# Hybrid retention / RG-LRU trunk: a new opening, a recurrent stage with input gates first, and seams freed tile by tile

## What is computed

```python
for l in range(2):
    sh1, sc1, g1, sh2, sc2, g2 = split(silu(cond) @ mod_w[l] + mod_b[l], 6)
    h = rmsnorm(x, norm_mix[l]) * (1 + sc1) + sh1
    if l == 0:   # four heads of bidirectional retention and a chunked spatial-gating MLP
        q, k, v, g, u, vv = split(h @ ab_w_in)
        mix = concat([o_ret, o_gm]) @ ab_w_out
    else:        # bidirectional RG-LRU, eight blocks of 128 channels
        gate_in, x_in = split(h @ lru_w_in, 2)
        xc = centred_dwconv(x_in)                       # 4 taps along the tokens
        r, ig = sigmoid(xc @ wa + ba), sigmoid(xc @ wx + bx)      # for each direction
        a = exp(-8 * r * softplus(-lam))
        h_d = scan(a, sqrt(1 - a * a) * (ig * xc))      # h[t] = a[t] h[t-1] + b[t]
        mix = (gelu(gate_in) * (h_f + h_b)) @ lru_w_out
    x = x + g1 * mix
    h = rmsnorm(x, norm_mlp[l]) * (1 + sc2) + sh2
    x = x + g2 * (square(relu(h @ mlp_w1[l])) @ mlp_w2[l])
y = rmsnorm(x, final_norm)
```

## Time and profile before

| | us |
|---|---|
| median of 3 runs | 2721.26 (2720.76 to 2726.55) |
| profiled execution, its own time | 2729.32 |
| its span | 2727.5 |
| PE busy | 2606.4 (96%) |
| DVE busy | 1641.2 (60%) |
| ACT busy | 666.5 (24%) |
| POOL busy | 700.0 (26%) |

### The profile page before, as it was taken

One profiled execution on the slowest core, in us unless ns is written; L12 is line 12 of the kernel. 1 busy time (PEld: TensorE's weight loads), 2 busy tenths in 40 slices (PEclk: granted clock), 3 DMA queues, 4 the chain that ended last, 5 costly groups with the idle time before them and its releaser, 6 DMA issues.

```text
span 2727.5 us, 39975 instructions
## 1 busy us (share of the span) xinstructions
PE 2606.4 (96%) x14730; PEld 2519.9 (92%) x14730; DVE 1641.2 (60%) x3056; ACT 666.5 (24%) x1016; POOL 700.0 (26%) x395
## 2 busy tenths in 40 slices
PE   8999999899999999999999889789999999999998
PEld 4999999899999999999998778678999999999998
DVE  5778778548567567567586776865433433343444
ACT  5323323232001001001044545423110110110113
POOL 0211212222222222222223232332223222232221
PEclk9999999999999999999999889899999999999999
DMA  6422222312222222222222101121111111111111
GB/s 229 149 74 68 83 64 74 124 47 64 65 81 69 63 83 69 62 85 69 62 74 104 38 19 38 44 84 39 43 43 39 46 38 46 38 39 46 38 46 70
DMA packets 259139, 181.18 MB, mean 66 GB/s; under 512 B 9205, under 2 KB 253685, under 8 KB 258166
## 3 DMA queue, kind: packets, MB, share of 16 engines
q1 hardware_dynamic: 257924, 169.99, 20.3%
q10 hardware_dynamic: 1138, 10.21, 1.0%
HBM read 165.48 MB, written 14.69 MB: 66 GB/s over the span
## 4 chain that ended last, share of the span: by engine, by line
PE 84%; DVE 10%; issue 3%; ACT 2%; DMA 0%; ACTq 0%; DVEq 0%; POOL 0%; POOLq 0%; SPq 0%
PE psum L588 79%; PE psum L862 2%; DVE mod_sum L1228 2%; DVE work_f L1624 1%; DVE h_lo L1254 1%; DVE sumsq L1197 1%; PE mod_psum L613 1%; DVE x L1275 1%; PE psum L668 1%; DVE sumsq L1260 1%; DVE h_hi L1598 1%; DVE mod_sum L1223 0%; DVE s_bwd L1474 0%; PE psum L743 0%; ACT rate_f L1107 0%
## 5 line engine op out<-in xcount | busy, mean ns | idle before, releaser
L588 PE MATMUL psum<-h_hi,w_hi 128*128 128x384 f32 (+1 forms) x2880 | 678.5, 344 | 37.1 <-DVE h_lo L1254 26.5
L531 POOL CAST w_hi<-w_raw 128x1024 fp32r<-128x1024 f32 x184 | 194.1, 1055 | 1881.6 <-PE psum L588 1028.0
L588 PE MATMUL psum<-h_lo,w_hi 128*128 128x384 f32 (+1 forms) x2880 | 663.1, 339 | 0.0
L588 PE MATMUL psum<-h_hi,w_lo 128*128 128x384 f32 (+1 forms) x2880 | 662.8, 338 | 0.0
L588 PEld LDWEIGHTS psum<-h_hi,w_hi 128*128 128x128 f32 x2880 | 517.9, 190 | 49.2 <-issue 23.1
L1275 DVE SCALAR_TENSOR_TENSOR x<-psum,mod,x 128x768 f32<-128x768 f32 (+2 forms) x432 | 238.5, 610 | 476.4 <-PE psum L588 476.4
L588 PEld LDWEIGHTS psum<-h_lo,w_hi 128*128 128x128 f32 x2880 | 521.9, 190 | 0.0
L588 PEld LDWEIGHTS psum<-h_hi,w_lo 128*128 128x128 f32 x2880 | 521.2, 190 | 0.0
L533 POOL TENSOR_TENSOR w_lo<-w_raw,w_hi 128x1024 fp32r<-128x1024 f32 x184 | 445.3, 2420 | 14.7
L978 ACT ACTIVATE relu<-relu,bias 128x384 f32<-128x384 f32 x128 | 72.0, 610 | 1207.5 <-DVE relu L1326 1207.5
L588 PE MATMUL psum<-hid_hi,w_hi 128*128 128x384 f32 x1536 | 351.9, 336 | 2.8 <-DVE x L1275 2.8
(11 more groups left out here) (223 smaller groups left out, 1888.5 us busy)
## 6 DMA issues: line engine op xcount, KB each, us to landing
w_raw<-in_mlp_w SPq DMA_DIRECT2D x128, 512.0 KB, 4.0
mod_raw<-in_mod_w SPq DMA_DIRECT2D x160, 256.0 KB, 2.9
w_raw<-in_ab_w_in SPq DMA_DIRECT2D x24, 512.0 KB, 4.6
x_spill<-x ACTq DMA_DIRECT2D x2, 4608.0 KB, 13.9
w_raw<-in_lru_w_in SPq DMA_DIRECT2D x16, 512.0 KB, 4.3
x<-x_spill SPq DMA_DIRECT2D x2, 2880.0 KB, 9.3
x_rows<-in_x_sample SPq DMA_DIRECT2D x8, 512.0 KB, 7.6
scale_raw<-in_mod_w SPq DMA_DIRECT2D x8, 512.0 KB, 14.4
```

The costliest lines, as they stand in the source:

```text
L531: pool.tensor_copy(w_hi[:, s, :], w_raw[:, s, :]).then_inc(hi_done, 1)
L588: mm = pe.matmul(psum[:, s, c, 0:end - c * CH], w, v[:, k, c * CH:end], start=(first and n == 0 and w is hi[k] and v is in_hi), stop=(last ...
```

## The change

Three parts change together.

1. Opening. PE begins with 10 matmuls on a tile of ones; SP loads four row blocks ahead of the parameters; rows are transposed as they land, with the parameters' transposes (`PAR_ITEM`) after the fifth. Squares are summed along rows on ACT (`row_squares`) and turned into `rstd` by three matmuls (`spread_rstd`) in place of seven adds and three long reciprocals on DVE. The modulation rows are multiplied with a 32-wide conditioning tile into four strips of 32 PSUM rows (`row_half`), scale in two halves ahead of the first unit, shift inside it after tile 5. `h_hi` and `h_lo` are made directly from `x` (`first_high`, `first_low`).
2. Recurrent stage. PE runs X of blocks 0 and 1 first, and then for each b: gates of b, G of b, X of b+2. The gates come as input gates of both directions, then recurrence gates. The products of gate and input move from POOL to DVE; one subtraction moves from DVE to ACT, beside the root. The last block has its gates ahead of the last G.
3. Seams. `mod_col(7)` of a head runs after the next head's first unit, or inside `out_proj(0)`. In the last unit before a seam PE signals each tile of `h` that it has passed (`free=`), and ACT, DVE and POOL overwrite that tile for the next stage at once. The MLP's `h` is written directly from `x` (`high_direct`, `low_direct`), without `gained`.

```diff
-            for n in range(2):
-                pe.wait_ge(par_landed[n], 16 * len(par_loads[n::2]))
+            keep_busy(WARM)
+            pe.wait_ge(consts_landed, 16)
+            for n in range(PAR_ITEM):
+                turn_rows(n)
...
+            def row_half(item, c, weights):
+
                 for k in range(KT):
+                    q = WIDE * (k % 4)
+                    last = pe.matmul(psum[q:q + WIDE, item % 2, c, :], cond_wide[:, k, :], weights(k), start=(k < 4), stop=(k >= 4))
+                return last
...
+                        if k == KT - 2:
+                            take_set(None, 0, SHIFT_ITEM)
+                            for m in range(KT):
+                                pe.wait_ge(shift_landed[m], 16)
+                            row_half(SHIFT_ITEM, 0, lambda m: shift_raw[m][:, 0:HALF * P])
+                            row_half(SHIFT_ITEM, 1, lambda m: shift_raw[m][:, HALF * P:KT * P]).then_inc(mini_done, 1)
...
                 big(0, 0).then_inc(unit_done, 1)
+                if not first_head(h):
+                    mod_column(h, HEAD_MODS, M0 - 1)
                 big(1, 1).then_inc(unit_done, 1)
...
-                mod_col(7)
...
+            project(None, 0, I1, 0, U1, *norm_waits(2)).then_inc(unit_done, 1)
+            project(None, 0, I1 + 1, 0, U1 + 1).then_inc(unit_done, 1)
+            with pe.Fori(0, KT - 2) as b:
+                gates(b)
+                project(b, BLK_ITEMS, I1 + BLK_G, BLK_UNITS, U1 + 2).then_inc(unit_done, 1)
+                project(b, BLK_ITEMS, I1 + BLK_NEXT_X, BLK_UNITS, U1 + 3).then_inc(unit_done, 1)
+            gates(KT - 2)
+            project(KT - 2, BLK_ITEMS, I1 + BLK_G, BLK_UNITS, U1 + 2).then_inc(unit_done, 1)
+            gates(KT - 1, True)
+            project(None, 0, I1 + LAST_G, 0, U1 + 2 * KT - 1, free=h_passed).then_inc(unit_done, 1)
...
+            def high_direct(n, k):
+
+                if k == 0:
+                    act.wait_ge(gain_ready, n + 2)
+                for t, c in tokens(x[:, k, :]):
+                    act.activation(h_hi[:, k, c * LAT:c * LAT + t.shape[1]], t, ACT.Copy, scale=gain[:, k, c:c + 1])
+                act.activation(h_hi[:, k, TOK:COLS], mod[:, n // 2, (SH1, SH2)[n % 2] + k, :], ACT.Copy).then_inc(part_hi, 1)
...
-                act.wait_ge(unit_done, AT_MLP[l].units)
                 for k in range(KT):
-                    if k == 4:
+                    if k < KT - 1:
+                        act.wait_ge(out_passed, l * (KT - 1) + k + 1)
...
-                    high_part(norm, k)
+                    high_direct(norm, k)
...
+                if last_head:
+                    act.wait_ge(gm_out, HEADS)
+                    for k in MIX_ORDER[0][:EARLY]:
+                        act.wait_ge(heads_passed, k + 1)
+                        mix_part(k)
...
+                act.wait_ge(scanned, at(b, 2, 2))
+                for j, (d, kind) in enumerate(GATE_ORDER):
...
+                    if j == 1 and not last_block:
+                        conv_bias(b, BLK_X)
...
+                if last_head:
+                    for n in range(EARLY_DVE):
+                        low_part(MIX_ORDER[0][n], mix[:, MIX_ORDER[0][n], :], H_MIX[0], n, TOK)
                 unit(5)
```

More of the change, by code:

```diff
@@ L106 @@
 DVE_LOW = 2
+EARLY_DVE, EARLY = 3, 6
 class Steps:
@@ L577, in take_set, with three_passes @@
                 return c % 2
-            def three_passes(s, tiles, hi, lo, in_hi, in_lo, width=TOK, first=True, last=True, before=None, behind=None):
+            def three_passes(s, tiles, hi, lo, in_hi, in_lo, width=TOK, first=True, last=True, before=None, behind=None,
+                             free=None):
                 for n, k in enumerate(tiles):
@@ L1030, in _, with head @@
             I0, U0, M0 = AT_MIX[0].items, AT_MIX[0].units, AT_MIX[0].minis
-            with act.Fori(0, HEADS) as h:
-                steps.enter(h, 9)
+            def head(h, last_head):
+                steps.enter(None if last_head else h, 9)
                 def mini(n):
@@ L1083, in _ @@
                 act.activation(by_bank(tile_of(mix, h)), whole(s), ACT.Copy).then_inc(read_out[s], 1)
-            steps.leave(HEADS)
+                steps.leave(1 if last_head else HEADS - 1)
+            with act.Fori(0, HEADS - 1) as h:
+                head(h, False)
+            head(HEADS - 1, True)
             out_proj(0)
@@ new lines, in mix_low, with lru_block @@
+            def mix_low(start, end):
+                for k in range(start, end):
+                    low_part(k, mix[:, k, :], H_MIX[1], k, TOK)
+            def lru_block(b, more):
+                steps.enter(b if more == 2 else None, 14 if more else 8)
+                for d in range(2):
+                    if more:
+                        item_out(dve, b, BLK_ITEMS, I0 + BLK_GATES + d)
+                    else:
+                        item_out(dve, None, 0, I0 + LAST_GATES + d)
+                    dve.tensor_tensor(gated[d][:], gated[d][:], xc[:], ALU.mult).then_inc(gated_ready, 1)
+                if more:
+                    convolution(b + 1)
@@ L1608, in lru_block @@
-                    after(steps.done())
-                    dve.scalar_tensor_tensor(out=work[d][:], in0=work[d][:], scalar=2.0, in1=work[d][:],
+                    dve.scalar_tensor_tensor(out=work[d][:], in0=rate[d][:], scalar=2.0, in1=rate[d][:],
                                              op0=ALU.subtract, op1=ALU.mult).then_inc(under_root, 1)
-                if not last_block:
-                    convolution(b, 1)
+                if more:
+                    output_gate(b, False)
+                else:
+                    mix_low(0, DVE_LOW)
@@ L1669, in constants @@
     table[:, C_KF], table[:, C_KB] = P - 1 - i, i
+    for j in range(2):
+        table[j::WIDE, C_SEL + j] = 1.0
     pos = np.arange(LAT)
```

541 lines of the change are left out of this document (335 added, 206 removed).

## The result

The changed kernel takes 2644.3 us (median of 4 runs, 2643.8 to 2644.7) against 2723.3 of the kernel before in the same comparison (2720.8 to 2726.6): a ratio of 0.9709, with a 95% interval of 0.9692 to 0.9726. That lies in the forecast range, 27 us above the point of 2617.

The account below looks back on a forecast made before the run. PE sets the end almost everywhere, losing time in few places. Savings of 53 (recurrent), 12 (heads), 6 (to out_proj(0)), 15 (MLP hand-overs) and 18 (opening) make 104 us: 2721.3 - 104 = 2617, with an 80% range of 2597 to 2646.

Parts of the forecast that it names:

- I take the differences off the median: Whole kernel: savings summed against the profiled execution of 2729.3 us were subtracted from the median of 2721.3.
- Recurrent stage: Seven recurrent blocks and the end behind them: period from 41.0 to 34.0 us, end 88 us, 53 us less.
- Opening: Before the network's first units: first unit starts at 32 instead of 59.8 us, ends at 58 instead of 77.8; 18 us less.
- the rival of serial strips: Opening: strips run one after another, each half 6.9 us and the shift 13.8; 2629 us, chance 18%.
- 24 + 3 + about 1.4 to read out and turn + 3: Opening: products begin at 24, two scale halves of 3.0 us with a read-out between; first tile of h ready about 31.4.
- Hand-overs to the MLPs: Both seams into an MLP, 22.9 and 23.1 us: work may begin 11 us earlier; 15 us less in both, ends 5 and 17.
- the seams give it back: Heads and both out_proj seams give nothing, the MLPs half, as waits move to DVE's next work; 2642 us, chance 12%.
- Heads: Three boundaries between heads: wait of 2.10 us for a modulation sum and 1.9 of half clock go; 12 us less.
- heads to out_proj(0): Seam from last head to out_proj(0), now 37.7 us: PE waits about 4 us behind the read-out; 6 us less, ends 0 and 11.
- the rivals in the recurrent stage: Recurrent blocks: DVE sets period 37.5, 2638 us, 15%; ring closes, 2747, 2%; order does nothing, 41.0, 2664, 1%.
- the ring: Recurrent blocks: ACT's and DVE's work strictly one after the other, period 54, slower than before at 2747 us; chance 2%.

Follow-up runs that it names:

- the two reorderings: Changed kernel with DVE's decay chain end behind the first gains and shift products a tile earlier, 2642.6 us; best version, also loading the second scale half earlier, 2622.2 us.
- hand-overs by column: Changed kernel, but at the four hand-overs ACT waits for the whole last column instead of tile by tile: 2655.6 us.
- seams reordered: Changed kernel with x's last tile updated after three low parts, last head's read-out ahead of three low parts, eighth modulation sum behind all: 2642.8 us.
- POOL's subtraction left out: Changed kernel, but POOL subtracts only 8 of 1,024 columns of each weight's low part from the third unit on: 2608.8 us in one run.
- the table early: Changed kernel with X of block b+2 read out directly behind the scans and ACT's table-loading sigmoid at the start of a block: 2635.3 us.
- X read out earlier: Changed kernel, but DVE reads X of block b+2 out directly behind the two scans, ahead of the sum of directions: 2641.1 us.
- POOL's split delayed: Changed kernel, but POOL splits the second unit's weights only when DVE's eight low parts of the opening are done: 2643.1 us.

## Why the forecast was right in the main and 27 us off

The 27 us have two parts. 8 are the step "I take the differences off the median": the rows came from an execution of 2729.3 us, and 2729.3 less 85 is 2644. Where that execution was 8 us longer than the median its rows do not tell; in the later rounds the kernel before has medians of 2726 to 2727 over 7 to 9 runs, so some 5 of the 8 may lie in a base of 3 runs. 19 are terms of the sum:

- *Recurrent stage*, 47 instead of 53. The period is 34.4 where 34.0 was forecast, because of a read-out behind a sum and a table load behind the gates. DVE is busy 185.6/6 = 30.9 us in a block and ACT 23.5 (29.5 and 22.5 forecast); I had given DVE back half of what POOL takes, and it got little of it. The gates of block 6 to column 2 of out_proj(1) take 92.5, not 88: the two waits stand where they were placed, 9.0 and 9.5 instead of 7.5. The step that was mis-sized is what DVE has queued ahead of a read-out, two products, two scans and two low parts; reordering it, with ACT's wait, gave 10.3 back.
- *Opening*, 12 instead of 18. The start of the products at 24 was right (24.05), and the rival of serial strips is refuted: 1.92 us a half where I took 3.0 (made serial, they cost 15 us where the rival had 12). One failed step is "24 + 3 + about 1.4 to read out and turn + 3": it counted the landing of the first half only. The second lands some 5 to 8 us later (products from 31.17 or 31.19 where nothing else held them, or from 29.35 where it was moved ahead), and the two reorderings show that advancing DVE, or that half, only brings up the next transfer. That is 4 us, a start at 35.9 instead of 32. The rest is lost behind the start: 29.6 us to the second unit where the forecast had 26 (32 to 58). It gave nothing for DVE and POOL holding each other up, for which PE waits 2.28 us here, and counted on the same tail as before, which ran at a granted clock of 1.00 then, where now the 9 us from the last tile to the second unit run mostly at 1.2 GHz. In two runs with the same opening, where DVE was not held up (hand-overs by column, seams reordered), these 29.6 us are 25.1 and 24.2, and the second unit starts 17 and 18 us earlier than before, not 12; for this stretch 19.8 were forecast, 1.5 of them given back in head 0. So most of the 6 us that are missing depend on which of the two engines comes first in an execution, and on the clock of the tail.
- *Hand-overs to the MLPs*, 8 instead of 15. The waits of the earlier trace rows did go, as the hand-overs by column show, but at mlp(1) there was no half clock to win, as the earlier trace rows has its clock at 1.00 before, and at both the last tile's update behind six low parts made a new one of 2.3. That is the MLPs' part of the rival "the seams give it back", half of the gain, as it said.
- *Heads*, 10.4 instead of 12 (3.1, 3.7 and 3.7 at the boundaries, for 4.0 each), and *heads to out_proj(0)*, 6.2 as forecast, with the wait behind the read-out at 3.5 (about 4 forecast).

Of the rivals in the recurrent stage none came: with all of DVE's work the period went down to 33.3, so neither DVE nor the ring sets it. The Trainium skill, "TensorE: Matmul & The Clock Gate", section "Why this matters for your kernels", gives 2.38 times for three strips, which made an estimate of 2.9 us a half; the run decides for 1.92, and 3.7 times for four strips.

## What to carry to other kernels

When a wait is taken from the bottleneck engine, look at what stands ahead of the next thing that it will wait for: here a read-out behind a sum, a table load behind a wait, a read-out behind a scan and a wait for two scans in place of one cost 17 us and were free to move. Where the neighbour's queue is truly full, as DVE's at the hand-overs to the MLPs, reordering only renames the wait. Before a stage's gain is put down to an edit, see whether that stage varies in runs that left it alone, as the opening does here. And take differences off the time of the execution from which the rows come.

## What the runs showed of the hardware

DVE and POOL hold each other up, and who is first is decided by a hair. In the changed kernel and five of the variants POOL's cast in the first unit ran in 1.04 to 1.26 us and DVE waited for POOL: twelve instructions of its low parts took 11.7 us. In three variants, whose opening is the same code (hand-overs by column, seams reordered, POOL's subtraction left out), the cast took over 5 us and DVE none the worse, 8.84; with the table early the cast took 2.10 and DVE 11.82 (timelines of POOL and DVE, first the changed kernel, then the seams reordered):

```profile
42.98 1.26 POOL L582 CAST w_hi<-w_raw 128x1024 fp32r<-128x1024 f32 x1 [14.31 <-DMA w_raw<-in_ab_w_in]
44.32 3.20 POOL L584 TENSOR_TENSOR w_lo<-w_raw,w_hi 128x1024 fp32r<-128x1024 f32 x1
```

```profile
38.87 11.71 DVE L1563 SCALAR_TENSOR_TENSOR h_lo<-x,gain,h_hi 128x1024 fp32r<-128x1024 f32 x12
```

```profile
43.08 5.33 POOL L582 CAST w_hi<-w_raw 128x1024 fp32r<-128x1024 f32 x1 [13.53 <-DMA w_raw<-in_ab_w_in]
...
38.67 8.84 DVE L1566 SCALAR_TENSOR_TENSOR h_lo<-x,gain,h_hi 128x1024 fp32r<-128x1024 f32 x12
```

These two casts start 0.1 us apart. Where the cast was held up, a long instruction of DVE (128x1024) had started 0.03 to 0.15 us ahead of it; where the cast went through, the next one started 0.02 to 0.27 us behind it. Where DVE won, the tail of the opening ended between 60.3 and 61.4 us, in the others between 64.6 and 66.3: a difference of some 5 us between executions of the same opening. The Trainium skill, "SBUF — State Buffer", section "SBUF: two separate sides", says that whichever of the two starts first holds their shared pair of ports for its whole instruction; these rows agree, and with the seams reordered DVE, once first, kept the cast off not for one instruction but until its run of low parts was over, at 47.5.

In the tail PE issues matmuls of two columns, busy all the time, and still falls to 1.2 GHz: the granted clock of the changed kernel is 1.00 from 54 to 58 us, 0.90 to 60 and 0.50 from there to 66. With the seams reordered the same instructions run at 1.00 throughout, and with X read out earlier as well, though there DVE was held up. With POOL's split delayed, PE had no wait in the unit and fell all the same, 0.70 from 60 to 62 us and 0.50 behind. What decides this is open.
